# Masking and scaling the probabilities of the second block's attention on other engines, ahead of their transposes

## The reference

```
o_slc, o_win = softmax(causal(q_rot k_slc^T)) v_slc, softmax(causal(q_rot k_win^T)) v_win
o_nsa = g0 * o_cmp + g1 * o_slc + g2 * o_win        # g = sigmoid(gates), one triple for each token and head
o_moba = softmax(causal(q k^T / 8)) v               # 8 heads, a single block of 256 keys
y = concat([o_nsa, o_moba]) @ w_out
```

## Time and profile before

| | us |
|---|---|
| median of 3 runs | 2136.75 (2136.4 to 2137.16) |
| profiled execution, its own time | 2137.32 |
| its span, first to last instruction | 2135.3 |
| TensorE busy | 2105.6 |
| POOL busy | 1621.3 |
| ScalarE busy | 1072.3 |
| VectorE busy | 791.4 |

### The profile page before, as it was taken

One profiled execution on the slowest core, in us unless ns is written; L12 is line 12 of the kernel. 1 busy time (PEld: TensorE's weight loads), 2 busy tenths in 40 slices (PEclk: granted clock), 3 DMA queues, 4 the chain that ended last, 5 costly groups with the idle time before them and its releaser, 6 DMA issues.

```text
span 2135.3 us, 36166 instructions
## 1 busy us (share of the span) xinstructions
PE 2105.6 (99%) x12792; PEld 1812.4 (85%) x12792; DVE 791.4 (37%) x1774; ACT 1072.3 (50%) x1809; POOL 1621.3 (76%) x686
## 2 busy tenths in 40 slices
PE   8999999999999999999999999999999999999998
PEld 7888988888888998888888887888888888788887
DVE  3224644223322545322322255532232225453223
ACT  5545544445545544554544465454455546445444
POOL 7887846888788865688788874668878887466886
PEclk9999999999999999999999999999999999999999
DMA  7555534555555543455555553445555554344553
GB/s 247 190 187 171 178 119 138 188 188 188 174 191 192 171 168 120 147 187 186 178 187 187 194 170 105 135 152 187 186 187 179 191 191 163 110 134 153 187 189 116
DMA packets 101140, 363.44 MB, mean 170 GB/s; under 512 B 11840, under 2 KB 12480, under 8 KB 100928
## 3 DMA queue, kind: packets, MB, share of 16 engines
q1 hardware_dynamic: 100624, 361.02, 51.3%
q10 hardware_dynamic: 432, 1.27, 0.2%
HBM read 361.20 MB, written 1.05 MB: 170 GB/s over the span
## 4 chain that ended last, share of the span: by engine, by line
PE 95%; DVE 2%; ACT 1%; issue 1%; DMA 0%; ACTq 0%; SPq 0%; DVEq 0%; POOLq 0%
PE twin L556 29%; PE twin L560 19%; PE twin L618 9%; PE twin L620 9%; PE twin L619 9%; PE twin L558 4%; PE twin L559 4%; PE twin L673 1%; PE twin L747 1%; PE twin L602 1%; PE twin L730 1%; PE twin L603 1%; PE twin L604 1%; PE twin L736 1%; PE twin L720 1%
## 5 line engine op out<-in xcount | busy, mean ns | idle before, releaser
L527 POOL TENSOR_TENSOR wlo<-raw,whi 128x1024 fp32r<-128x1024 f32 x682 | 1621.1, 2405 | 498.5 <-ACT whi L1226 498.1
L1226 ACT CAST whi<-raw 128x1024 fp32r<-128x1024 f32 x682 | 696.7, 1052 | 81.1 <-PE twin L560 29.4
L560 PE MATMUL twin<-turned,wlo 128*128 128x256 f32 x1968 | 550.4, 280 | 0.0
L556 PE MATMUL twin<-early,whi 128*128 128x512 f32 x1344 | 479.6, 398 | 0.5
L556 PE MATMUL twin<-turned,whi 128*128 128x512 f32 x1344 | 473.5, 395 | 1.3 <-DVE turned L1584 1.2
L560 PE MATMUL twin<-early,wlo 128*128 128x256 f32 x1536 | 431.0, 281 | 0.0
L1644 DVE TENSOR_TENSOR twin<-twin,mix 128x512 f32<-128x512 f32 x168 | 117.4, 699 | 757.0 <-ACT mix L1285 757.0
L560 PEld LDWEIGHTS twin<-turned,wlo 128*128 128x128 f32 x1968 | 372.8, 189 | 3.7
L1285 ACT COPY mix<-twin 128x512 f32<-128x512 f32 x168 | 98.6, 587 | 438.1 <-PE twin L560 438.1
L556 PEld LDWEIGHTS twin<-early,whi 128*128 128x128 f32 x1344 | 252.4, 188 | 65.3 <-issue 2.0
L556 PEld LDWEIGHTS twin<-turned,whi 128*128 128x128 f32 x1344 | 252.6, 188 | 60.9 <-issue 1.6
(11 more groups left out here) (292 smaller groups left out, 2203.3 us busy)
## 6 DMA issues: line engine op xcount, KB each, us to landing
raw<-in_w_dram SPq DMA_DIRECT2D x682, 512.0 KB, 3.3
con<-in_con_dram ACTq DMA_DIRECT2D x1, 1161.5 KB, 7.7
x<-in_x_dram SPq DMA_DIRECT2D x2, 512.0 KB, 7.1
out_dram<-xs SPq DMA_DIRECT2D x4, 256.0 KB, 2.8
mix<-in_last_gain_dram SPq DMA_DIRECT2D x1, 512.0 KB, 4.4
par<-in_par_dram SPq DMA_DIRECT2D x2, 208.0 KB, 3.4
par<-in_par_dram SPq DMA_DIRECT2D x2, 154.0 KB, 3.2
con<-in_con_dram ACTq DMA_DIRECT2D x1, 64.0 KB, 3.8
```

The costliest lines, as they stand in the source:

```text
L527: nc.gpsimd.tensor_tensor(wlo[:, place, :], raw[:, place, :], whi[:, place, :].bitcast(F32), ALU.subtract).then_inc(split_done, 1)
L556: pe.matmul(out, hi, both.rearrange("p c n -> p (c n)"), start=start and k == 0, stop=False, skip_group_check=True)
L560: mm = pe.matmul(out[:, 0:SEQ], lo, both[:, 0, :], start=False, stop=stop and k == KD - 1, skip_group_check=True)
L1226: nc.scalar.copy(whi[:, place, :], raw[:, place, :]).then_inc(hi_done, 1)
```

## The change

The mask is no longer a matmul. VectorE adds it to the two diagonal blocks of both score banks in one instruction ahead of the maxima. The factors (gate over row sum) are computed as soon as the exponentials are done (`pair_factors`), and ScalarE scales the probabilities with them in place (`pair_normal`, four copies with a scale), in the iteration after the exponentials. The transposes follow two chunks after the scores, and the weighing in the same chunk as the transposes. P has room for three pairs. As the scale is already in the probabilities, the selected and the windowed branch of a head pair accumulate in one PSUM bank, `spread` and R go, and ScalarE copies the finished sums (`sums_kept`). The later addition of the two branches goes too. `gates_turned` moves from chunk 8 to chunk 7. The second mixer does not call `set_masks` any more.

Core of the diff:

```diff
-TURNED = {9: 0, 10: 1, 11: 2, 12: 3, 14: 4, 15: 5, 16: 6, 17: 7, 19: 8, 24: 9, 27: 10, 28: 11}
-WEIGHED = {9: 0, 10: 1, 11: 2, 12: 3, 14: 4, 16: 5, 17: 6, 18: 7, 19: 8, 24: 9, 27: 10, 28: 11}
-GATES_TURNED, HID0_TURNED, KC_DONE, CMP_SCORED, CMP_TURNED = 8, 19, 21, 22, 25
+TURNED = {c + 2: p for c, p in SCORED.items()}
+GATES_TURNED, HID0_TURNED, KC_DONE, CMP_SCORED, CMP_TURNED = 7, 19, 21, 22, 25
...
+def sums_begin(p):
+
+    return p >= 8 or p % 2 == 0
+
+
+def sums_end(p):
+
+    return p >= 8 or p % 2 == 1
+
+
+def sums_of(p):
+
+    return "o", p // 2 if p < 8 else p - 4
...
-            t.add(("o", WEIGHED[c]), 4)
+        if c in TURNED and sums_begin(TURNED[c]):
+            t.add(sums_of(TURNED[c]), 4)
...
-            ("P", 1536), ("pt", 1536), ("nm", 8), ("rowsum", 8), ("fac", 8), ("R", 256), ("ywin", 1024),
+            ("P", 2304), ("pt", 1536), ("nm", 8), ("rowsum", 8), ("fac", 8),
...
+        def probs_of(p, h):
+
+            at = (p % 3 * 2 + h) * 384
+            return m2("P", 2304)[:, at:at + 384]
...
-                    pe.matmul(out[half_rows(h), 0:SEQ], value(h, 0), turned(h)[:, 0:SEQ], start=True, stop=False, skip_group_check=True)
+                    pe.matmul(out[half_rows(h), 0:SEQ], value(h, 0), turned(h)[:, 0:SEQ], start=first, stop=False, skip_group_check=True)
...
-                    if p == 0:
-                        pe.wait_ge(ev("mask_ready"), L.each)
-                    for h in range(2):
-                        mask_scores(out[h], maskR[:])
                     for h in range(2):
                         rows = slice(HD * h, HD * h + HD)
-                        pe.matmul(out[h][:, 0:P], q[rows, 0:P], k[rows, 0:P], start=False, stop=False, skip_group_check=True)
+                        pe.matmul(out[h][:, 0:P], q[rows, 0:P], k[rows, 0:P], start=True, stop=False, skip_group_check=True)
...
-                    out = claim(pe, L, ("o", p))
+                    out = claim(pe, L, sums_of(p)) if sums_begin(p) else psum(L, sums_of(p))
                     wait_drained(pe, L, ("ip", VSW if p < 8 else MV0 if p < 10 else MV1))
                     for h in range(2):
                         wait_drained(pe, L, ("pt", p, h))
-                    pe.wait_ge(ev("fac_ready"), L.l * PAIRS + (p + 1))
-                    weigh(out, lambda h, T: value(p, h, T), lambda h: m2("pt", 1536)[:, (p % 2 * 2 + h) * 384:(p % 2 * 2 + h + 1) * 384])
-                    factor = lambda t, T, h: m2("fac", 8)[:, p % 2 * 4 + T * 2 + h:p % 2 * 4 + T * 2 + h + 1]
-                    full(L, ("o", p), spread(out[:, SEQ:2 * SEQ], factor, 1))
+                    turned = lambda h: m2("pt", 1536)[:, (p % 2 * 2 + h) * 384:(p % 2 * 2 + h + 1) * 384]
+                    mm = weigh(out, lambda h, T: value(p, h, T), turned, sums_begin(p))
+                    if sums_end(p):
+                        full(L, sums_of(p), mm)
...
-                        turn_probs(L, TURNED[c], m2("P", 1536)[:, TURNED[c] % 2 * 768:(TURNED[c] % 2 + 1) * 768])
+                        p = TURNED[c]
+                        pe.wait_ge(ev("probs_ready"), L.l * PAIRS + (p + 1))
+                        turn_probs(L, p, m2("P", 2304)[:, p % 3 * 768:(p % 3 + 1) * 768])
...
-                    if c in WEIGHED:
-                        weighted(WEIGHED[c])
+                    if c in TURNED:
+                        weighted(TURNED[c])
...
+                def pair_normal(p):
+
+                    act.wait_ge(ev("fac_ready"), L.l * PAIRS + (p + 1))
+                    for h in range(2):
+                        pr = probs_of(p, h)
+                        for T, cols in ((0, slice(0, P)), (1, slice(P, 3 * P))):
+                            f = p % 2 * 4 + T * 2 + h
+                            ins = nc.scalar.activation(pr[:, cols], pr[:, cols], ACT.Copy, scale=m2("fac", 8)[:, f:f + 1])
+                    ins.then_inc(ev("probs_ready"), 1)
+
+                def sums_kept(p):
+
+                    at = p // 2 if p < 8 else p - 8
+                    wait_full(act, L, sums_of(p))
+                    drained(L, sums_of(p), nc.scalar.copy((y_sum if p < 8 else y_moba)[:, at * SEQ:(at + 1) * SEQ], psum(L, sums_of(p))[:, 0:SEQ]))
...
-                    if c - 1 in WEIGHED:
-                        p = WEIGHED[c - 1]
-                        wait_full(act, L, ("o", p))
-                        nc.scalar.copy(m2("R", 256), psum(L, ("o", p))[:, SEQ:2 * SEQ]).then_inc(ev("r_copied"), 1)
+                    if c - 1 in TURNED and sums_end(TURNED[c - 1]):
+                        sums_kept(TURNED[c - 1])
                     for m in TAKEN.get(c, ()):
                         taken(m)
                     if c >= AHEAD:
                         split_hi(L, FFN_SLOTS + c + AHEAD)
+                    if c - 1 in SCORED:
+                        pair_normal(SCORED[c - 1])
                     if c in SCORED:
                         pair_exps(SCORED[c])
...
-                set_masks()
...
+                    ends = S.rearrange("p h (b n) -> p h b n", b=2)[:, :, :, 0:P]
+                    own.link(dve.tensor_tensor(ends, ends, bc(c_("negq").unsqueeze(1).unsqueeze(1), [P, 2, 2, P]), ALU.add))
                     dve.tensor_reduce(m2("nm", 8)[:, f:f + 2], S[:, :, 0:P], AX, ALU.max, negate=True)
                     dve.tensor_reduce(m2("nm", 8)[:, f + 2:f + 4], S[:, :, P:3 * P], AX, ALU.max, negate=True).then_inc(sm_max, 1)
...
-                def pair_kept(p):
+                def pair_factors(p):
 
                     kind, r = pair_of(p)
                     f = slice(p % 2 * 4, p % 2 * 4 + 4)
-                    fac, kept = m2("fac", 8)[:, f], [m2("pt", 1536)[:, (p % 2 * 2 + h) * 384:(p % 2 * 2 + h + 1) * 384] for h in range(2)]
-                    wait_full(dve, L, ("pt", p, 0))
-                    drained(L, ("pt", p, 0), dve.tensor_copy(kept[0], psum(L, ("pt", p, 0))[:, 0:384]))
+                    fac = m2("fac", 8)[:, f]
                     for h in range(2):
                         wait_drained(dve, L, ("s", p, h))
-                    wait_full(dve, L, ("pt", p, 1))
                     if kind == "moba":
                         dve.reciprocal(fac, m2("rowsum", 8)[:, f]).then_inc(ev("fac_ready"), 1)
-                    else:
-                        spare = psum(L, ("pt", p, 1))[:, 384:388]
-                        own.link(dve.reciprocal(spare, m2("rowsum", 8)[:, f]))
-                        at = 8 * (1 + (kind == "win")) + r
-                        dve.tensor_tensor(two(fac), two(spare), g4[:, :, at:at + 5:4], ALU.mult).then_inc(ev("fac_ready"), 1)
-                    drained(L, ("pt", p, 1), dve.tensor_copy(kept[1], psum(L, ("pt", p, 1))[:, 0:384]))
-
-                def outputs(p):
-
-                    kind, r = pair_of(p)
-                    dve.wait_ge(ev("r_copied"), L.l * PAIRS + (p + 1))
-                    dst = {"slc": y_sum, "win": m2("ywin", 1024), "moba": y_moba}[kind][:, r * SEQ:(r + 1) * SEQ]
-                    drained(L, ("o", p), dve.tensor_tensor(dst, psum(L, ("o", p))[:, 0:SEQ], m2("R", 256), ALU.mult))
+                        return
+                    own.link(dve.reciprocal(fac, m2("rowsum", 8)[:, f]))
+                    at = 8 * (1 + (kind == "win")) + r
+                    dve.tensor_tensor(two(fac), two(fac), g4[:, :, at:at + 5:4], ALU.mult).then_inc(ev("fac_ready"), 1)
+
+                def pair_kept(p):
+
+                    for h in range(2):
+                        wait_full(dve, L, ("pt", p, h))
+                        kept = m2("pt", 1536)[:, (p % 2 * 2 + h) * 384:(p % 2 * 2 + h + 1) * 384]
+                        drained(L, ("pt", p, h), dve.tensor_copy(kept, psum(L, ("pt", p, h))[:, 0:384]))
...
-                    if c - 1 in WEIGHED:
-                        outputs(WEIGHED[c - 1])
...
-                    if c in (20, 22):
-                        wait_drained(dve, L, ("o", 7))
-                        at = slice((c - 20) * 256, (c - 20) * 256 + 512)
-                        own.step(dve.tensor_tensor(y_sum[:, at], y_sum[:, at], m2("ywin", 1024)[:, at], ALU.add))
                     if c == 28:
                         remainders_of_y(0, 4, y_moba[:, 0:512]).then_inc(ev("y_split"), 1)
                     if c == 30:
                         remainders_of_y(1, 6, y_moba[:, 512:1024]).then_inc(ev("y_split"), 1)
+                    if c in SCORED:
+                        pair_factors(SCORED[c])
...
+                        wait_drained(dve, L, sums_of(7))
                         for j in range(2):
                             wait_full(dve, L, ("cmp_o", j))
-                            own.wait()
```

More of the change, by code:

```diff
@@ L731, in turn_probs, with weigh @@
                     full(L, ("pt", p, h), mm)
-            def weigh(out, value, turned):
+            def weigh(out, value, turned, first=True):
                 for h in range(2):
-                    pe.matmul(out[half_rows(h), 0:SEQ], value(h, 0), turned(h)[:, 0:SEQ], start=True, stop=False, skip_group_check=True)
```

(7 more changed lines are left out.)

## The result

The changed kernel takes 2145.07 us (median of 6 runs, 2143.76 to 2148.02), the kernel before beside it 2137.11 (2136.4 to 2137.56): a ratio of 1.0038, 95% interval 1.0027 to 1.0049. It is slower by 8 us. Forecast were 2133.8 us and a range of 2128 to 2140. The profiled execution is the fastest of the six, 2143.76 with a span of 2142.0.

What follows compares the result with a forecast made beforehand. TensorE, busy 99% of the span, was taken as the bound. Of 21 to 23 us removed, each mixer kept 0.3 + 4.1 - 2.6 = 1.8, less 0.3: 3.0 us over two, giving 2133.8 us; range 2128 to 2140.

Steps and rivals of the forecast that it cites:

- Step (f): Chunks 19 to 26: nothing waits, two masks and two spreads saved, 1.9 us; lead 4.1 at the last scores.
- Step (g): Tail: last scores to TensorE's restart after L2067 take 15.8 us instead of 13.2, a loss of 2.6.
- The clock rival: Wait ahead of chunk 15's scores drops TensorE to 1.2 GHz; 3 us twice, 6 us, 2140; chance 0.04.
- (d): Chunks 13 to 15: TensorE idle 2 to 2.7 us ahead of chunk 15's scores; lead 2.8 at the cast, 1.4 after.
- Step (e): Chunks 15, 16, 18: waits of 0.7 us each, 4.5 per pair against 4.3 to 4.8 before; lead 2.2 at end.
- (b): Chunks 8 to 10: gates ahead of first scores, a 0.7 us wait; chunk 11's scores come 2.0 us earlier.
- (a): Before the mixer: removed mask casts no longer stand in front of L1614; gain 0.3 us.
- (c): Chunk 11: 0.97 us removed bring 0.3; 1.8 us wait before L730; lead 2.8 with chunk 12's spread gone.
- dear-mask rival: VectorE's mask addition is dear: each 0.1 us costs 1.2 over both mixers; no gain from 1.0 us; chance 0.14.
- rival of short waits: TensorE's idle time is half of what the walk finds: saving 13 us, 2124; with none, 2114; chance 0.20.

Runs made afterwards that it cites:

- e7: Changed kernel with the compressed softmax's sums and factors in PSUM, order unchanged; 2141.9 us, ratio 1.0027.
- e9: Kernel before plus six unused constant copies on ScalarE in chunk 14, between its cast and pair 5's exponentials; 2143.7 us, ratio 1.0032.
- e12: Changed kernel with e7's edit and, in chunk 14 alone, normalising ahead of ScalarE's cast; 2137.5 us, ratio 0.9999.
- e11: Changed kernel with VectorE's copy of the second hidden block ahead of the last remainders instead of behind them; 2140.4 us, ratio 1.0017.
- e3: Changed kernel with VectorE's causal mask addition left out; 2137.0 us, ratio 0.9998.
- e6: Kernel before with only the mask moved from TensorE's matmuls to an addition on VectorE; 2136.7 us, ratio 0.9997.
- e2: Changed kernel with ScalarE normalising ahead of its cast in chunk 24 alone; 2142.6 us, ratio 1.0025.
- e5: Changed kernel with the mask put back on TensorE's matmuls, all else kept; 2144.4 us, ratio 1.0037.
- e8: Changed kernel reordered only: normalising ahead of the cast in six chunks, some weighing a chunk later, last pair a chunk earlier; 2130.6 us, ratio 0.9967.
- e10: Changed kernel with e8's order plus the edits of e7 and e11; 2123.6 us, ratio 0.9941.
- e1: Changed kernel with the four normalising copies ahead of the copy of sums, projections' copies and cast in every chunk; 2141.5 us, ratio 1.0021.
- e4: Changed kernel with the four normalising copies on ScalarE left out, probabilities unscaled; 2137.3 us, ratio 1.0002.

## Why the prediction was wrong

Per mixer 1.5 us of gain was forecast and the first one of the profile lost 4.08 (158.06 to 162.14), the second 3.3. Of the 5.6 us between in the first:

- **Step (f) failed**: "Chunks 19 to 26 are long, nothing waits". TensorE had slack there; VectorE had met POOL. With the transposes and kept copies of pair 9 gone from chunk 24, the softmax came 3.5 us earlier in the mixer and POOL's subtractions 0.8, POOL started 0.05 us ahead of the first product, and 2.0 us were lost in chunk 25 (e7 removes exactly that). Step (g) of the same text had reckoned with POOL for the remainders; step (f) didn't ask what else on VectorE has two operands in SBUF.
- **The clock rival was priced and placed, then dismissed**: 0.04, since "waits of 2 us around chunk 4 brought no lower level". The trace of the kernel before has no such wait: behind its first ones, at the start, the longest of TensorE up to the end is 0.9 us. The lower level came behind the wait of (d), and others, and cost 1.7 us in each mixer of the profiled run, where 3 was priced (e9 and e12 have falls of 3.4). There is more of it in three of the six runs, which step from 2144.0 over 2146.3 to 2148.0 as their clock goes from 0.997 over 0.996 to 0.995. e9 shows that the wait alone does it. With 0.9965 in the middle against 0.998 to 0.999 before, the term is 0.002 x 2140, some 4 us of the 8 lost, as far as three digits of the clock tell.
- **Step (e) promised too much**: 2.2 us of lead at its end were forecast, 1.0 is measured at the start of chunk 19. Its 4.8 us for a pair before runs to 1328.41 and so holds the transposes of pair 8, which the changed kernel still has to make (0.6); and a pair costs 4.7 in place of 4.5, since the kept copies land 3.9 behind the scores in place of 3.8, and the weighing takes 0.80 to the start of what stands behind it now, where it took 0.70 to the spread. Step (f) gained 1.2 in e7 in place of 1.9; where its 0.7 went was not taken apart. In e7, where neither meeting nor fall comes in, the lead at the last scores is 2.2 where 4.1 was forecast: 1.9 us, and the mixer is 0.4 longer than before in place of 1.5 shorter.

1.9 + 2.0 + 1.7 = 5.6. What held: (b) (2.4 us of lead at the scores of chunk 11; forecast 2.0, and 2.3 with the 0.3 of (a)), (c) (a wait of 1.6 for 1.8; a lead of 3.1 at the scores of chunk 13 for 2.8, or 3.1 with (a)), (d) (2.8 us of wait for 2 to 2.7, and a lead of 1.4 behind it; 1.7 with (a), and the 0.3 that is short is what the forecast had taken off for late ends), and (g) (15.8 us from the last scores to the restart, as forecast; e11 takes the wait away). The mask addition took 0.69 to 0.70 us, with its link 0.72, and the four normalising copies 1.40 from start to next: the dear-mask rival is out, and e3 and e6 show what the cheap one costs all the same. The waits of TensorE rose by 11.5 us in the first mixer (4.1 to 15.6) where about 10 was forecast, and 2.0 of them are the meeting: the rival of short waits is out as well.

Open: which wait brings a fall in a given execution. The profiles show them behind waits of 2.8 (after in its second mixer, e2, e3, e5, e9, e11), 2.0 (after, e11), 1.7 (e8, not e10, whose wait is the same) and in the tail (e1 to e5, e8, e12), while the same 2.8 us wait passed without one in e7's profile and in the first mixer after. Of the fourteen waits of 2.8 us in the profiles of these kernels nine have a fall behind them, of the six of 2.0 us in chunk 25 two. The shortest wait with a fall behind it is the 1.7 us of e8. Each kernel has one profile, so these counts are small, and no run shows what decides. The Trainium skill, TensorE: Matmul & The Clock Gate, What's actually happening, has the clock set by how busy the engine was lately, and that agrees with e9, where nothing but six copies on ScalarE and the wait for them were added.

## What to carry to other kernels

When work is taken from the engine that bounds and given to others, the first question is no longer its sum but where each new wait lies: here 21 to 23 us removed became 8 us lost, the same instructions in another order 6.7 us gained, and with two small edits more 13.5. Walk the schedule for every engine, and mark each instruction of VectorE with both inputs in SBUF against POOL's intervals (and small ones with one input, such as L2145): a shift of 3 us put them on each other here, and one operand in PSUM parted the two products from POOL. Count a wait of TensorE like those above (1.7 to 2.9 us) at its length plus a fall of the clock that may follow, and read the spread of the runs against their granted clock before the medians.

## What the runs showed that was not expected

A product of 16 columns took 2.37 us beside a subtraction of POOL, thirteen times its 0.18. A wait of 2.8 us added to a kernel whose mixers had kept the upper clock level sent it to the lower one in both of them, for 1.7 to 3.4 us of loss each, while waits up to 1.5 us (e6) did not. And the same kernel can differ by 9 us between executions along with the clock: e7's runs at a mean of 0.999 and 0.993.
